# Expert stage of a hybrid decoder step: an item of token slots goes from 128 to 112

## The reference, cut to what matters

```
def moe_swiglu(h, router_w, w1, w3, w2):        # h: 320 tokens x 1024
    logits = (t @ router_w)                     # 320 x 8
    top_v, top_i = lax.top_k(logits, 2)
    gates = jax.nn.softmax(top_v, axis=-1)
    for e in range(8):                          # w1[e], w3[e]: 1024 x 3584; w2[e]: 3584 x 1024
        w_e = jnp.sum(jnp.where(top_i == e, gates, 0.0), axis=-1)
        out = out + w_e[:, None] * ((silu(t @ w1[e]) * (t @ w3[e])) @ w2[e])
```

## Time and profile before

| | us |
|---|---|
| median of 3 runs | 1541.67 |
| lowest, highest | 1540.67, 1543.83 |
| span of the profiled execution | 1539.8 |

### The profile page before, as it was taken

How to read it: one execution, slowest core, us unless ns; L and a number is a source line. 1 busy time by engine, 2 the same in 40 slices (tenths; PEclk the granted TensorE clock), 3 DMA queues, 4 the chain that set the end, 5 groups by cost and what they waited for, 6 DMA issues and landing times.

```text
span 1539.8 us, 21793 instructions
## 1 busy us (share of the span) xinstructions
PE 1520.4 (99%) x8105; PEld 1294.0 (84%) x8105; DVE 1189.0 (77%) x971; ACT 946.2 (61%) x723; POOL 94.9 (6%) x133
## 2 busy tenths in 40 slices
PE   8999999999999999999999999999999999999997
PEld 6787999999977888888888888888888888888885
DVE  4686454444476869898888888888888888889997
ACT  3454423332344557677777777777777777777774
POOL 3220000000002023000000000000000000001001
PEclk9999999999999999999999999999999999999999
DMA  9997944444447859999999999999999999999993
GB/s 351 387 358 268 374 143 157 137 163 137 163 170 296 269 185 361 354 393 394 375 376 387 381 375 388 374 378 378 393 371 385 376 380 374 377 375 374 401 394 122
DMA packets 235378, 492.59 MB, mean 320 GB/s; under 512 B 10155, under 2 KB 16171, under 8 KB 231226
## 3 DMA queue, kind: packets, MB, share of 16 engines
q1 hardware_dynamic: 227110, 472.82, 83.4%
q0 software_dynamic: 5920, 18.57, 3.2%
q10 hardware_dynamic: 2308, 0.64, 0.2%
HBM read 481.86 MB, written 10.36 MB: 320 GB/s over the span
## 4 chain that ended last, share of the span: by engine, by line
PE 95%; DVE 2%; DMA 2%; ACT 1%; SPq 1%; issue 0%; ACTq 0%; DVEq 0%
PE ps L1784 20%; PE ps L1786 20%; PE ps L1785 20%; PE ps L2200 4%; PE ps L2202 4%; PE ps L2201 4%; PE ps L1812 2%; PE ps L2211 2%; PE ps L2212 2%; PE ps L2210 2%; PE ps L2348 2%; PE ps L2154 1%; PE ps L2155 1%; PE ps L2156 1%; PE ps L1917 1%; PE ps L1829 1%
## 5 line engine op out<-in xcount | busy, mean ns | idle before, releaser
L1138 DVE TENSOR_TENSOR w_lo<-raw,w_hi 128x2048 fp32r<-128x2048 f32 x366 | 835.2, 2291 | 172.4 <-ACT w_hi L762 171.1
L762 ACT ACTIVATE w_hi<-raw 128x2048 fp32r<-128x2048 f32 x366 | 701.6, 1917 | 257.7 <-PE ps L1786 161.1
L1784 PE MATMUL ps<-w_hi,split 128*128 128x512 f32 x1392 | 549.0, 394 | 0.6 <-DVE w_lo L1138 0.5
L1786 PE MATMUL ps<-w_hi,split 128*128 128x512 f32 x1392 | 542.5, 390 | 0.0
L1785 PE MATMUL ps<-w_lo,split 128*128 128x512 f32 x1392 | 541.9, 389 | 0.0
L1784 PEld LDWEIGHTS ps<-w_hi,split 128*128 128x128 f32 x1392 | 261.4, 188 | 58.7 <-DVE w_lo L1138 4.3
L1786 PEld LDWEIGHTS ps<-w_hi,split 128*128 128x128 f32 x1392 | 261.3, 188 | 55.3
L1785 PEld LDWEIGHTS ps<-w_lo,split 128*128 128x128 f32 x1392 | 261.6, 188 | 51.7
L2200 PE MATMUL ps<-split,w_hi 128*128 128x320 f32 x432 | 133.8, 310 | 0.0
L2202 PE MATMUL ps<-split,w_lo 128*128 128x320 f32 x432 | 133.5, 309 | 0.0
L2201 PE MATMUL ps<-split,w_hi 128*128 128x320 f32 x432 | 133.5, 309 | 0.0
(11 more groups left out here) (368 smaller groups left out, 1306.7 us busy)
## 6 DMA issues: line engine op xcount, KB each, us to landing
raw<-in_moe_w SPq DMA_DIRECT2D x336, 1024.0 KB, 7.3
raw<-in_ffn_w SPq DMA_DIRECT2D x42, 1024.0 KB, 5.0
raw<-in_ada_w SPq DMA_DIRECT2D x40, 1024.0 KB, 8.9
raw<-in_w_in SPq DMA_DIRECT2D x12, 1024.0 KB, 9.2
raw<-in_ada_w SPq DMA_DIRECT2D x16, 512.0 KB, 11.2
raw<-in_w_out SPq DMA_DIRECT2D x8, 1024.0 KB, 10.3
item_rows<-plain POOLq DMA_DIRECT2D x12, 512.0 KB, 7.8
plain<-in_x_prompt SPq DMA_DIRECT2D x2, 512.0 KB, 3.7
```

The source lines that it names most:

```text
L762: a.activation(w_hi[:, (s0 + j) % SPL], raw[:, (u0 + j) % RAW], ACT.Copy).then_inc(hi_ready, 1)
L1138: v.tensor_tensor(w_lo[:, (s0 + j) % SPL], raw[:, (u0 + j) % RAW], w_hi[:, (s0 + j) % SPL].bitcast(F32), ALU.subtract).then_inc(lo_ready, 1)
L1784: t_.matmul(out, a_hi, b_hi, start=first_, stop=False)
L1786: return t_.matmul(out, a_lo, b_hi, start=False, stop=last_)
```

## The change

`CAP` = 112 slots for each item take the place of `P` = 128 wherever slots are meant: thresholds of the counts, places, tables, rows of `item_rows`, the fetch. In `e_up` and `e_down` the stationary operands are 112 columns and the sums 112 partitions. The transposes of `xs_tok` and `e_g` read 112 rows and move 112 columns of the identity; the splits of their results take 4 x 112 of each 4 x 128 elements. Elementwise work on rows of tokens takes 112 partitions. Buffers in SBUF and the layout in PSUM keep their strides of 128. `EXTRA_MAX` goes from 4 to 5, so `item_rows` has 13 x 112 rows for 12 x 128.

```diff
+CAP = 112
-EXTRA_MAX = 4
+EXTRA_MAX = 5
...
-    d['item_rows'] = nc.dram_tensor("item_rows", (NI * P, D), F32, kind="Internal").ap()
+    d['item_rows'] = nc.dram_tensor("item_rows", (NI * CAP, D), F32, kind="Internal").ap()
...
-                    gp.dma_start(d['item_rows'][e * P:(e + 1) * P, :], zero_rows).then_inc(zero_out, 16)
+                    gp.dma_start(d['item_rows'][e * CAP:(e + 1) * CAP, :], zero_rows[0:CAP]).then_inc(zero_out, 16)
...
-        step(g.tensor_scalar(ext[:], cnt[:], float(P), None, ALU.is_gt))
+        step(g.tensor_scalar(ext[:], cnt[:], float(CAP), None, ALU.is_gt))
...
-            gp.indirect_dma_start(xs_tok, None, d['tok_rows'],
-                                  bass.IndirectOffsetOnAxis(ap=idx_now[:, 0:1], axis=0)).then_inc(gath, 16)
+            gp.indirect_dma_start(xs_tok[0:CAP], None, d['tok_rows'],
+                                  bass.IndirectOffsetOnAxis(ap=idx_now[0:CAP, 0:1], axis=0)).then_inc(gath, 16)
...
-            gp.dma_start(d['item_rows'][bass.ts(i, P), :], e_y).then_inc(y_out, 16)
+            gp.dma_start(d['item_rows'][bass.ts(i, CAP), :], e_y[0:CAP]).then_inc(y_out, 16)
...
-                a.activation(out, ps[:, 2, :].rearrange("p (a b) -> p a b", b=P), ACT.Copy).then_inc(e_hi, 1)
+                a.activation(out[:, :, 0:CAP], ps[:, 2, :].rearrange("p (a b) -> p a b", b=P)[:, :, 0:CAP], ACT.Copy).then_inc(e_hi, 1)
...
-                v.tensor_tensor(e_g[:], e_silu[:], ps[:, 1, :], ALU.mult).then_inc(e_mu, 1)
+                v.tensor_tensor(e_g[0:CAP], e_silu[0:CAP], ps[0:CAP, 1, :], ALU.mult).then_inc(e_mu, 1)
...
-                    ins = t_.matmul(ps[:, XS_BANK0[half], k * P:(k + 1) * P], htok[0:n, b, at:at + P], oh0[0:n, b, :],
+                    ins = t_.matmul(ps[:, XS_BANK0[half], k * P:k * P + CAP], htok[0:n, b, at:at + P], oh0[0:n, b, 0:CAP],
...
-                    ins = t_.transpose(ps[:, XS_BANK[half], k * P:(k + 1) * P], xs_tok[:, at:at + P], ident[:])
+                    ins = t_.transpose(ps[:, XS_BANK[half], k * P:k * P + CAP], xs_tok[0:CAP, at:at + P], ident[0:CAP, 0:CAP])
...
-                    ins = mm3(ps[:, bank, :], xs_hi[:, kk, :], xs_lo[:, kk, :], w[0][:, k, :], w[1][:, k, :],
+                    ins = mm3(ps[0:CAP, bank, :], xs_hi[:, kk, 0:CAP], xs_lo[:, kk, 0:CAP], w[0][:, k, :], w[1][:, k, :],
...
-                    ins = t_.transpose(ps[:, 2, m * P:(m + 1) * P], e_g[:, m * P:(m + 1) * P], ident[:])
+                    ins = t_.transpose(ps[:, 2, m * P:m * P + CAP], e_g[0:CAP, m * P:(m + 1) * P], ident[0:CAP, 0:CAP])
...
-                    ins = mm3(ps[:, 3 + c, :], gh[:, k, :], gl[:, k, :], w[0][:, k, :], w[1][:, k, :],
+                    ins = mm3(ps[0:CAP, 3 + c, :], gh[:, k, 0:CAP], gl[:, k, 0:CAP], w[0][:, k, :], w[1][:, k, :],
...
-                t_.matmul(ps[0:n, LAST_BANK[b][c], :], sel, ey_hi[:, cols], start=False, stop=False)
+                t_.matmul(ps[0:n, LAST_BANK[b][c], :], sel, ey_hi[0:CAP, cols], start=False, stop=False)
```

More of the change, by code:

```diff
@@ L674, in _ @@
         gp.wait_ge(rk_ready, 1)
-        step(g.tensor_scalar(ext2[:], cnt[:], float(2 * P), None, ALU.is_gt))
-        step(g.tensor_scalar(ext[:], cnt[:], float(P), None, ALU.is_gt))
+        step(g.tensor_scalar(ext2[:], cnt[:], float(2 * CAP), None, ALU.is_gt))
+        step(g.tensor_scalar(ext[:], cnt[:], float(CAP), None, ALU.is_gt))
         step(g.tensor_tensor(ext[:], ext[:], ext2[:], ALU.add))
@@ L681, in _ @@
         step(g.tensor_tensor(ext2[:], ebase[:], ext[:], ALU.add))
-        step(g.tensor_scalar(eoff[:], ebase[:], float(P), None, ALU.mult))
+        step(g.tensor_scalar(eoff[:], ebase[:], float(CAP), None, ALU.mult))
         step(g.tensor_tensor(eoff[:], eoff[:], later_by[:], ALU.add))
@@ L718, in _ @@
         gp.wait_ge(y_cp, last_item + 1)
-        gp.dma_start(d['item_rows'][bass.ts(last_item - 1, P), :], e_y).then_inc(y_out, 16)
+        gp.dma_start(d['item_rows'][bass.ts(last_item - 1, CAP), :], e_y[0:CAP]).then_inc(y_out, 16)
         def fetch_outputs(b, j, y, arrived):
@@ L1040, in xs_split_hi @@
                 act.wait_ge(xs_tr, n + half)
-                a.activation(xs_hi[:, half * KB:(half + 1) * KB, :],
-                             ps[:, banks[half], :].rearrange("p (b c) -> p b c", c=P), ACT.Copy).then_inc(xhi, 1)
+                a.activation(xs_hi[:, half * KB:(half + 1) * KB, 0:CAP],
+                             ps[:, banks[half], :].rearrange("p (b c) -> p b c", c=P)[:, :, 0:CAP], ACT.Copy).then_inc(xhi, 1)
         xs_split_hi(1, XS_BANK0)
@@ L1056, in e_silu_step @@
                 act.wait_ge(e_mu, i * NSTEP + 1 if s is None else i * NSTEP + s + 1)
-                a.activation(e_silu[:], ps[:, 0, :], ACT.Silu).then_inc(e_si, 1)
+                a.activation(e_silu[0:CAP], ps[0:CAP, 0, :], ACT.Silu).then_inc(e_si, 1)
             def gt_split(n, out):
                 act.wait_ge(e_tr, n)
-                a.activation(out, ps[:, 2, :].rearrange("p (a b) -> p a b", b=P), ACT.Copy).then_inc(e_hi, 1)
+                a.activation(out[:, :, 0:CAP], ps[:, 2, :].rearrange("p (a b) -> p a b", b=P)[:, :, 0:CAP], ACT.Copy).then_inc(e_hi, 1)
             e_up(2)
@@ L1081, in e_item @@
                     act.wait_ge(split_used, i * N_FFN + (S_MOE + N_FFN - 1 + c))
-                    a.activation(ey_hi[:, c * B:(c + 1) * B], ps[:, 3 + c, :], ACT.Copy).then_inc(last_hi, 1)
+                    a.activation(ey_hi[0:CAP, c * B:(c + 1) * B], ps[0:CAP, 3 + c, :], ACT.Copy).then_inc(last_hi, 1)
                 return
@@ L1090, in e_item @@
             act.wait_ge(y_free, i + 1)
-            a.activation(e_y[:, 0:B], ps[:, 3, :], ACT.Copy)
+            a.activation(e_y[0:CAP, 0:B], ps[0:CAP, 3, :], ACT.Copy)
             act.wait_ge(split_used, i * N_FFN + (S_MOE + N_FFN))
-            a.activation(e_y[:, B:D], ps[:, 4, :], ACT.Copy).then_inc(y_cp, 1)
+            a.activation(e_y[0:CAP, B:D], ps[0:CAP, 4, :], ACT.Copy).then_inc(y_cp, 1)
         e_item(0, False)
@@ L1538, in _ @@
         v.tensor_tensor(tokid[:], tokid[:], pidx[:, 0:1].unsqueeze(1).to_broadcast([P, 2, NBLK]), ALU.add)
-        v.tensor_scalar(thr[:], iota[:, 0:NI + 3], float(P), None, ALU.mult)
-        v.tensor_scalar(own[:], iota[:, 0:E], float(P), None, ALU.mult)
-        step(v.tensor_scalar(later_by[:], iota[:, 0:E], -float(P), float(P * (E - 1)), ALU.mult, ALU.add))
+        v.tensor_scalar(thr[:], iota[:, 0:NI + 3], float(CAP), None, ALU.mult)
+        v.tensor_scalar(own[:], iota[:, 0:E], float(CAP), None, ALU.mult)
+        step(v.tensor_scalar(later_by[:], iota[:, 0:E], -float(CAP), float(CAP * (E - 1)), ALU.mult, ALU.add))
         v.tensor_copy(s_sel[0:ROWS].rearrange("p (b t) -> p b t", t=TS),
@@ L1602, in xs_split_lo @@
                 ve.wait_ge(xhi, n + half)
-                v.tensor_tensor(xs_lo[:, part_k, :], ps[:, banks[half], :].rearrange("p (b c) -> p b c", c=P),
-                                xs_hi[:, part_k, :].bitcast(F32), ALU.subtract).then_inc(xlo, 1)
+                v.tensor_tensor(xs_lo[:, part_k, 0:CAP], ps[:, banks[half], :].rearrange("p (b c) -> p b c", c=P)[:, :, 0:CAP],
+                                xs_hi[:, part_k, 0:CAP].bitcast(F32), ALU.subtract).then_inc(xlo, 1)
         xs_split_lo(1, XS_BANK0)
@@ L1611, in find_places @@
             v.tensor_tensor(posn[:], rank[:], own[:].unsqueeze(1).to_broadcast([P, NBLK, E]), ALU.add)
-            step(v.scalar_tensor_tensor(out=over1[:], in0=rank[:], scalar=float(P),
+            step(v.scalar_tensor_tensor(out=over1[:], in0=rank[:], scalar=float(CAP),
                                         in1=eoff[:].unsqueeze(1).to_broadcast([P, NBLK, E]), op0=ALU.is_ge, op1=ALU.mult))
@@ L1622, in find_places @@
             step(v.tensor_reduce(item_no[:], at_least[:, :, 1:NI + 3], AX.X, ALU.add))
-            step(v.scalar_tensor_tensor(out=slot_no[:], in0=item_no[:], scalar=-float(P), in1=places,
+            step(v.scalar_tensor_tensor(out=slot_no[:], in0=item_no[:], scalar=-float(CAP), in1=places,
                                         op0=ALU.mult, op1=ALU.add))
@@ L1682, in e_mul @@
                     ve.wait_ge(e_si, i * NSTEP + s + 1)
-                v.tensor_tensor(e_g[:], e_silu[:], ps[:, 1, :], ALU.mult).then_inc(e_mu, 1)
+                v.tensor_tensor(e_g[0:CAP], e_silu[0:CAP], ps[0:CAP, 1, :], ALU.mult).then_inc(e_mu, 1)
             def gt_split(n, hi_part, out):
                 ve.wait_ge(e_hi, n)
-                v.tensor_tensor(out, ps[:, 2, :].rearrange("p (a b) -> p a b", b=P),
-                                hi_part.bitcast(F32), ALU.subtract).then_inc(e_lo, 1)
+                v.tensor_tensor(out[:, :, 0:CAP], ps[:, 2, :].rearrange("p (a b) -> p a b", b=P)[:, :, 0:CAP],
+                                hi_part[:, :, 0:CAP].bitcast(F32), ALU.subtract).then_inc(e_lo, 1)
             def e_step(s):
@@ L1736, in _ @@
             e_item(item, False)
-        step(v.tensor_scalar(last_at[:], tab[:, EXTRA_MAX:], -float(P), float(P), ALU.mult, ALU.add))
```

(9 more changed lines are left out.)

## The result

The changed kernel takes 1547.45 us (median of 7 runs, 1544.6 to 1548.39) against 1541.43 us of the kernel before (7 runs, 1540.46 to 1543.83). The ratio is 1.0032, 95% interval 1.0021 to 1.0042: 6 us slower, where 3.7 us faster was forecast with a range up to 1543.

A forecast was written before the change was run, and what follows sets the result against it. TensorE, busy 99% of the span, was taken to bound the kernel; the transposes' 3.7 us was the only gain, all other terms zero, so 1541.67 - 3.7 = 1537.9 us, range 1531 to 1543.

The forecast's parts named there:

- The number of items: Expert stage: still 8 items, as the largest expert has 110 tokens, under 112; no time change.
- the tail: Last selection, ey_hi and ey_lo: rows fall away, 512 elements and 512 moved columns stay; zero.
- the transfers: Fetched and stored rows 1/8 fewer, with a whole item of 118 us for them; zero.
- the first item's tokens: L2311, 48 fp32 products moving 112 columns, paced by the 128-column load that stays: zero, at most 48 x 13.3 ns = 0.6 us.
- The 4032 products: Expert products with 112 stationary columns: load hidden, pitch stays 226.7 ns, zero; ends of the range -53.6 and +20 us.
- rival D: Loads under 128 columns add a fixed amount at each of 4032 products; at 2.5 ns, 1548.0 us; chance 0.07.
- The transposes: 280 transposes in TensorE's stream move 112 columns instead of 128, 13.3 ns less each: 3.7 us gained.
- The waits: TensorE's 2.5 us of waits for VectorE stay, as shorter splits give VectorE about 53 ns a step.
- The weight load: Load of a product's stationary operand: some 175 ns for 112 columns, 188 for 128, hidden beside the running product.

The follow-up runs named there:

- experiment 1: The changed kernel with the expert products back at 128 stationary columns, all else at 112: 1540.61 us, ratio 0.9989 to the kernel before.
- experiment 2: The kernel before with only the expert products at 112 stationary columns, transposes, splits and items at 128: 1553.89 us, ratio 1.0074.
- experiment 7: The kernel before with 112 stationary columns in the dense stage's up and down products, 320 columns moved: 1541.33 us, ratio 1.0.
- 9 to 12: The kernel before, expert products moving 448 columns with 112 or 128 stationary, 320 with 112, 384 with 96: intervals 200.0, 202.9, 146.6, 174.2 ns; times not read.
- experiment 4: The kernel before with 64 stationary columns in the expert products: 1553.24 us, ratio 1.0061.
- 8: Full products of 128 columns as in experiment 1, with 120 in place of 112 in the transposes: 1540.59 us, ratio 0.9998 to the kernel before.

## Why the prediction was wrong

**The number of items, the tail, the transfers, the first item's tokens**: as forecast; nothing of the loss lies there.

**The 4032 products**: this step failed. "For an eighth fewer columns I take zero" had 2.4 ns in its place (229.5 less 227.1 ns, averages over the stage): 228.9 ns in most settled runs and 233.3 in some, where the pitch was to stay at 226.7. The direct measure in us is the changed kernel against experiment 1, which differs in nothing but these columns: the stage takes 954.9 us against 947.9, so they cost 7.0 us. The rest of the change gained 2.5 us (947.9 against 950.4), which makes the +4.5 us of the stage; the medians of the runs grew by 6.0. The sum by averages agrees roughly: 2.4 ns x 4032 = 9.7 us, less the 3.7 us forecast for the transposes, less 1.9 us of waits that went (2.5 to 0.6 us), +4.1. The price was inside the bounds of the step (up to 5 ns) and of rival D (2.5 ns, 1548.0 us), but the rival had a chance of 0.07. It was not quite rival D's mechanism: no fixed surcharge on a load under 128 columns, since 320 and 448 moved columns with 112 stationary pay none. It goes by the pair of stationary and moved columns. Experiment 1 shows that the products' columns cause the loss, 2 that they do so alone, 7 and 9 to 12 that the width moved decides as much.

**How the rows were misread**: the step rested on three products of 64 columns and their twins of 128, 235 ns apart both the earlier trace rows. The twins of 128 should have been 226.7 ns apart, as in every settled run of the stage. They were not, and the tail has a second set of such twins, which the prediction didn't use:
```profile
1526.16 0.39 PE L2415 MATMUL ps<-split 128*128 128x512 f32 x1
...
1526.62 0.40 PE L2415 MATMUL ps<-split 128*128 128x512 f32 x1
```
They are 231 ns apart (462 ns for two). So the control alone scatters between 231 and 235 ns and is far from its known value both times. That these products come too soon behind other work to have settled fits what stands behind the transposes, but no run shows it for the tail. Settled, 64 columns cost 3.3 ns (experiment 4: 230.0 for 226.7), which a pair of such short stretches could not show. The row carried its own warning: a control that doesn't show the known value is not a control.

**The transposes**: the single term was right (12 in 1.15 us, 96 ns each; rows 10 to 12 read rightly), and in the changed kernel 49 of its 53 ns a step have arrived when the second product behind the transposes starts. With full products they don't pay as much. Experiment 1 has only 39 ns at that point; "that the following product's load is shorter too [...] lets it keep up" fits this, though load and product were put back together there. It then loses 17 ns in the eleven intervals behind, which the sum had left out, so 53 ns become some 23 in a step: 2.5 us in the stage and a ratio of 0.9989 (0.9979 to 0.9999) for the whole in place of 3.7 us.

**The waits**: nearly right. VectorE kept up; TensorE's waits for it did not stay at 2.5 us but fell to 0.6, as the stream got slower.

**The weight load**: it was forecast at 175 ns and took 174, where it had taken 188. By the Trainium skill, "TensorE: Matmul & The Clock Gate", section "LDWEIGHTS (loading the stationary operand)", a load of P columns takes P / 1.2 ns, so 16 columns fewer are 13.3 ns by an estimate from that page; the trace agrees with 14. The load got shorter and the stream got longer: that a load is hidden beside a product doesn't make the size of its operand free.

**Open**: why some pairs settle at streaming + 13.3 ns and others 2 to 7 ns above, and what puts a run at 112 columns into one of its two rhythms. Whether the load's columns or the result's partitions count wasn't separated, since one `matmul` sets both. The pattern repeats regularly within a stretch (three intervals long at 112 columns, four at 96: 228, 229, 231, 232 ns) while VectorE and ScalarE start and stop beside it, which speaks for TensorE itself and against the other engines, but no run shows it.

The version of experiment 1 (112 slots everywhere but in the products) has the lowest ratio of those that compute the whole result: 1540.61 us, 0.1% below the kernel before, with an interval that just excludes no change.

## What to carry to other kernels

Where products stand back to back, the interval of starts is the cost, and it belongs to the pair of stationary and moved columns: measure the new pair itself, and don't take it for granted that fewer columns are at worst free. A settled stretch of some twenty products tells more than a few behind other work; check first that the control shows the known value. Take the mean over many runs of products as well, since one pair can have two rhythms and a single stretch shows one of them. After a shortened instruction in such a stream, look at those behind it too: they may give the gain back.

## What the runs showed of the hardware that was not expected

- 512 moved columns: 226.7 ns with 128 stationary, 230.0 with 96 and with 64, 233.3 with 120. With 112 there are two rhythms, 228.9 and 233.3 ns: 40 and 4 of 44 long runs in the changed kernel, 27 and 15 of 42 in experiment 2.
- 448 moved: 200.3 ns with 112 stationary, 203.2 with 128. 320 moved: 146.7 ns with 128 and with 112, though the single intervals differ (experiment 7).
- Mixing 128, 128 and 112 stationary columns is slower (231.2 ns on average) than 112 throughout (230.7, with transposes of 128 beside both).
- Products of 128 stationary columns right behind transposes take 4 to 5 ns more each on average (single ones up to 9) before they are at 226.7 ns, at an unchanged clock of 1.00: six intervals in the kernel before, nine in experiments 1 and 8, counted from the second product.
